# Router logits in four column strips, and steps of the routing moved forward, in a one-core mixer and MoE kernel

## The chip, the cores and the metric

The kernel runs on one core of one Trainium2 chip. The metric is the device time of one execution in microseconds (us).

## The reference

One layer for two sequences, 128 context tokens and 512 latent tokens, with 1024 channels in float32. Each token gets an adaLN-modulated norm, a mixer (mLSTM heads beside a Hyena group, joined by one output projection) and then a hierarchical mixture of 16 experts. What matters here stands between the mixer and the experts:

```python
def rms_norm(x, g):
    y = xf * lax.rsqrt(jnp.mean(xf * xf, axis=-1, keepdims=True) + EPS)
    return y * g
...
x = x + g1 * rms_norm(y, p['g_norm'][1])                  # y: the mixer's output
h = rms_norm(x, p['g_norm'][2]) * (1.0 + sc2) + sh2       # what router and experts read
...
p_coarse = softmax(xt @ p['w_rc'] + p['b_rc'])            # 4 groups, top 1
p_grp, g_idx = lax.top_k(p_coarse, 1)
l_fine = (xt @ p['w_rf'] + p['b_rf']).reshape(t, N_GROUPS, EXPERTS_PER_GROUP)
...
top_l, e_idx = lax.top_k(l_sel, TOP_K_FINE)               # top 2 of the group's 4 experts
w_sel = jax.nn.softmax(top_l, axis=-1) * p_grp
```

So the router has 4 + 16 = 20 logits per token, each a sum over 1024 channels.

## The kernel before, in words

The program is written by hand for each engine, with semaphores `S[...]` between them: TensorE (`pe`), ScalarE (`act`), VectorE (`dve`), GpSimd (`pool`, which issues DMAs) and SyncE (`sp`, which issues the weight loads). `mem` is the SBUF arena ("arena" in the profile), `ps` the eight PSUM banks of 512 float32 columns ("banks"). The 640 tokens are five tiles of 128; the output stage takes them in the order `out_tiles = [0, 3, 2, 4, 1]`, and `j` is the place in that order.

The output stage, about 484 to 563 us of the profiled execution, does for each tile j:

- TensorE: `turn_heads(j)` transposes the heads (L1841), `out_hyena(j)` (L1856) and `out_mlstm(j)` (L1866) form y in two banks, `turn_x2` transposes x2 (L1876), and `logits` (L1887) multiplies h2T, as weights of 128x128, with `wrt` of 20 columns, eight products into 20 columns of bank 7. A float32 product is two instructions. TensorE's order in the loop is `turn_heads(j)`, `turn_x2(j - 2)`, `out_hyena(j)`, `logits(j - 2)`, `out_mlstm(j)`: the logits of a tile come two tiles later. Those of the last two tiles follow after the loop, and then `stay_busy(3)`, products whose result is used by nobody.
- ScalarE: `out_norm(j)` squares both halves of y (L808) and takes the root of their sum (L811); `x2_norm(j)` does the same with x2 (L816, L817); `x2_columns(j, c)` copies the transposed x2 into `h2T` (L823).
- VectorE: `residual(j)` adds the two sums (L1280), takes the reciprocal (L1282) and forms x2 (L1285, L1286); `expert_rows(j)` takes the second reciprocal (L1293) and makes the expert input in two passes of 128x1024 (L1296 multiplies by the norm and a row, L1297 adds a row), which GpSimd's queue stores to DRAM. For the last tile VectorE copies the second half of h2T itself (L1312).

The norm of x2 is not in the logits: they are formed from x2 as it is, with `wrt` scaled by the modulation (L1176, at about 380 us), and VectorE multiplies by the norm when it reads them (L1351).

Then the routing: VectorE sets constants (L1334 to L1339), waits for the logits of all tiles, and finds groups, experts and places, with a few products of TensorE in between (L1917 to L1941, the latter with the 0/1 matrix `fold` that adds four parts of 32 lanes). GpSimd gathers the first rows (L533), and TensorE goes through the groups of 32 tokens, sorted by expert: `gate_and_up` (L1961) and `down` (L1972), with a transpose between (L1980). These use column strips: the weights are 32 tokens, four products stand side by side in the array, and each writes its own quarter of the partitions. SyncE loads the weights of 16 experts in order into three sets of buffers: those of expert 1 after `wo_done` (all tiles projected), of expert 2 after `h2_ready`, of expert e + 3 when expert e is done.

Of the kernel before, what the change touches and what calls it, by code (L numbers as in the profile page):

```python
# [9 lines left out]
ALU = mybir.AluOpType  # L10
ACT = mybir.ActivationFunctionType
# [92 lines left out]
def emit(nc, a, stack):  # L104
# [113 lines left out]
    wrt_lat, wrt_ctx = area(rows1_at, KD, 20), area(cpad_at, KD, 20)  # L218
    shift_sums = area(cpad_at + 160, 2, 20)
# [27 lines left out]
    rbias5 = area(W6 + 960, NT, 20)  # L247
    shifted = area(W1b + 3592, 2, KD, 20)
# [24 lines left out]
    def rt(*shape):  # L273
# [33 lines left out]
        h_ready hsq hss hrs yml_ready yt_done yt_read wo_done wo_sq wo_ss wo_rs x2_sq x2_rs h2_ready h2t_done h2t_read  # L307
# [267 lines left out]
    def _(act):  # L575
# [229 lines left out]
        def out_norm(j):  # L805
            for c in range(2):
                act.wait_ge(S["wo_done"], 2 * j + c + 1)
                link(A(squares[:, c * CH:(c + 1) * CH], ps[:, 1 + 2 * (j % 2) + c, :], ACT.Square,  # L808
                       accum_out=st1[:, 20 + 2 * j + c:21 + 2 * j + c]), "wo_sq")
            act.wait_ge(S["wo_ss"], j + 1)  # L810
            link(A(st1[:, 30 + j:31 + j], st1[:, 30 + j:31 + j], ACT.Sqrt, bias=epsc, scale=1.0 / D), "wo_rs")  # L811
# [7 lines left out]
        def x2_columns(j, c):  # L819
            act.wait_ge(S["h2t_done"], 2 * j + c + 1)  # L820
            if j >= 2:
                act.wait_ge(S["lg_done"], j - 1)
            link(A(h2T[:, j % 2, 4 * c:4 * c + 4, :], ps[:, 5 + c, :].rearrange("p (k t) -> p k t", t=P), ACT.Copy),  # L823
                 "h2t_read")

# [5 lines left out]
        for j in range(NT - 1):  # L831
            x2_norm(j)
            if j == 2:
                out_norm(3)
            for c in range(2):
                x2_columns(j, c)
            if j + 3 < NT:
                heads_square(j + 3)
                heads_root(j + 3)
            if j != 2:  # L840
                out_norm(j + 1)
        x2_columns(NT - 1, 0)
        x2_norm(NT - 1)

# [54 lines left out]
    def _(dve):  # L899
# [275 lines left out]
        for g, scaled in enumerate((wrt_ctx, wrt_lat)):  # L1175
            link(TT(scaled, wrt, pack[:, 1, g, :].unsqueeze(2).broadcast_to((P, KD, 20)), ALU.mult))  # L1176
            link(TT(shifted[:, g], wrt, pack[:, 2, g, :].unsqueeze(2).broadcast_to((P, KD, 20)), ALU.mult))
            link(dve.tensor_reduce(shift_sums[:, g, :], shifted[:, g].rearrange("p k n -> p n k"), AX_X, ALU.add),
                 "consts_ready" if g else "dve_chain")
# [90 lines left out]
        def residual(j):  # L1270
# [7 lines left out]
            dve.wait_ge(S["wo_sq"], 2 * j + 2)  # L1278
            s = st1[:, 30 + j:31 + j]
            link(TT(s, st1[:, 20 + 2 * j:21 + 2 * j], st1[:, 21 + 2 * j:22 + 2 * j], ALU.add), "wo_ss")  # L1280
# [6 lines left out]

        def expert_rows(j):
            t = out_tiles[j]
            rows = row_ctx if t == 0 else row_lat  # L1290
            s = st1[:, 35 + t:36 + t]
            dve.wait_ge(S["x2_rs"], j + 1)
            link(dve.reciprocal(s, s))  # L1293
            if j >= 2:
                dve.wait_ge(h2_stored[j % 2], 16 * (j // 2))
            link(STT(tbuf, x2[:, t, :], s, rows[1], ALU.mult, ALU.mult))  # L1296
            link(TT(h2buf[j % 2], tbuf, rows[2], ALU.add), "h2_ready")  # L1297
# [26 lines left out]
        def over(x, *dims):  # L1324
            return x.broadcast_to((P,) + dims)

# [6 lines left out]
        for coef in (g_coef, e_coef, t_coef):  # L1333
            link(dve.memset(coef, 1.0))  # L1334
            link(dve.memset(coef[:, :, 0:1], 0.0))
        link(dve.tensor_reduce(fold[:, 0:LANE], ident.rearrange("p (q r) -> p r q", q=LANES), AX_X, ALU.add))
        link(CP(fold[:, LANE:].rearrange("p (q r) -> p q r", r=LANE), over(fold[:, 0:LANE].unsqueeze(1), LANES - 1, LANE)))
        link(dve.memset(used, 15.5 / P))
        link(dve.memset(cum, 1.0))  # L1339

# [8 lines left out]
        dve.wait_ge(S["lg_done"], NT)  # L1349
# [135 lines left out]
    def _(pe):  # L1485
# [394 lines left out]
        def logits(j):  # L1880
            t = out_tiles[j]
            w = wrt_lat if t else wrt_ctx
# [14 lines left out]
        for j in range(2, NT):  # L1897
# [3 lines left out]
            logits(j - 2)  # L1901
# [3 lines left out]
        logits(NT - 2)  # L1905
        turn_x2(NT - 1)
        logits(NT - 1)


        def stay_busy(n):  # L1910

            for _ in range(n):
                M(ps[:, 0, :], ident, x2[:, 0, 0:CH], start=True, stop=True)

# [112 lines left out]
```

## Time and profile before

| | us |
|---|---|
| median of three executions | 893.09 (892.60 to 893.87) |
| the profiled execution | 892.52 |
| its span, first to last instruction | 890.7 |
| TensorE busy | 812.8 (91%) |
| VectorE busy | 416.4 (47%) |
| ScalarE busy | 273.8 (31%) |
| GpSimd busy | 105.2 (12%) |

The profile's page sums up one execution. Its views of the trace are the chain of work that ended last (each step followed back to what released it), the timeline of an engine (instructions in order of time, those of one line merged, with the idle time before and what ended it), busy times by stretch with the clock granted to TensorE (1.00 is 2.4 GHz, 0.50 is 1.2 GHz), and the DMA issues with the time to their landing. "x16" is a count of instructions. The time between the span and the execution's own is 1.8 us.

### The profile page before, as it was taken

How to read it: one execution, taken by the hardware profiler on the slowest of the kernel's cores; microseconds unless marked ns; L12 is line 12 of the kernel's file. 1: busy time of each engine (PE TensorE's matmuls, PEld its weight loads, DVE VectorE, ACT ScalarE, POOL GpSimd, SP SyncE). 2: the span in 40 equal slices, each digit the busy share in tenths (PEclk: the TensorE clock that was granted, in tenths of full speed). 3: DMA queues.
4: the chain of work that ended last, by engine and by line, in shares of the span. 5: the costliest groups of instructions: out<-in, count | busy, mean ns of one | idle time of the engine just before them, and what ended most of it. 6: DMA issues, size and time to landing. Idle time of an engine off the chain costs nothing.

```text
span 890.7 us, 17116 instructions
## 1 busy us (share of the span) xinstructions
PE 812.8 (91%) x6809; PEld 442.7 (50%) x6809; DVE 416.4 (47%) x761; ACT 273.8 (31%) x549; POOL 105.2 (12%) x205
## 2 busy tenths in 40 slices
PE   5998999999999999998998999789999999999930
PEld 1242455554554457455764555455555555555510
DVE  5546531123881681753554674733333333333328
ACT  1666321123110311246222233113333333333315
POOL 4000000000001000001001000122222222222131
PEclk9999999999999999998999999699999999999975
DMA  7967450213054503043009204989999999996145
GB/s 256 413 258 273 161 216 0 95 44 146 1 189 149 138 0 107 14 137 100 1 22 368 83 24 183 411 343 416 417 422 419 414 420 419 414 423 281 49 132 239
DMA packets 40201, 191.40 MB, mean 215 GB/s; under 512 B 4416, under 2 KB 4712, under 8 KB 32529
## 3 DMA queue, kind: packets, MB, share of 16 engines
q1 hardware_dynamic: 29146, 155.12, 43.7%
q0 software_dynamic: 8448, 28.99, 9.5%
q10 hardware_dynamic: 2552, 6.50, 2.1%
q8 instruction: 42, 0.69, 0.3%
q14 instruction: 13, 0.11, 0.0%
HBM read 174.14 MB, written 16.44 MB: 214 GB/s over the span
## 4 chain that ended last, share of the span: by engine, by line
PE 82%; DVE 7%; ACT 4%; issue 3%; DMA 2%; POOL 0%; SPq 0%; POOLq 0%; DVEq 0%; ACTq 0%
PE banks L1961 19%; PE banks L1622 16%; PE banks L1972 9%; PE banks L1623 4%; PE banks L1866 4%; PE banks L1856 4%; PE banks L1584 3%; PE banks L1762 3%; PE banks L1771 3%; PE banks L1516 2%; PE banks L1563 2%; ACT arena L763 2%; PE banks L1654 2%; PE banks L1727 2%; PE banks L1980 1%
## 5 line engine op out<-in xcount | busy, mean ns | idle before, releaser
L1961 PE MATMUL banks<-arena 128*32 128x256 f32 x3072 | 175.7, 381 | 1.6 <-DVE arena L1438 1.6
L1622 PE MATMUL banks<-arena 128*128 128x512 f32 x320 | 164.2, 595 | 1.5 <-issue 0.8
L1961 PEld LDWEIGHTS banks<-arena 128*32 128x32 f32 x3072 | 96.2, 110 | 64.7 <-issue 2.6
L1623 PEld LDWEIGHTS banks<-arena 128*128 128x128 f32 x320 | 60.8, 190 | 76.4 <-issue 76.4
L1438 DVE STREAM_TRANSPOSE arena<-arena 128x256 f32<-128x256 f32 x49 | 32.1, 656 | 137.9 <-PE banks L1961 131.5
L1972 PE MATMUL banks<-arena 128*32 128x256 f32 x1536 | 91.7, 379 | 1.0 <-DVE arena L1462 1.0
L1972 PEld LDWEIGHTS banks<-arena 128*32 128x32 f32 x1536 | 50.3, 110 | 33.5 <-DVE arena L1462 1.2
L1623 PE MATMUL banks<-arena 128*128 128x128 f32 x320 | 61.5, 274 | 0.0
L1445 DVE COPY arena<-banks 32x256 f32<-32x256 f32 x98 | 41.4, 422 | 40.8 <-PE banks L1972 40.1
L857 ACT ACTIVATE arena<-banks 32x256 f32<-32x256 f32 x98 | 36.6, 374 | 71.5 <-PE banks L1972 70.9
L1622 PEld LDWEIGHTS banks<-arena 128*128 128x128 f32 x320 | 48.6, 192 | 4.8 <-issue 3.3
L543 POOL DMA_INDIRECT arena<-expert_input,arena x47 | 46.2, 984 | 12.5 <-issue 12.5
L1016 DVE SCALAR_TENSOR_TENSOR arena<-banks,arena 128x504 f32<-128x504 f32 x12 | 8.9, 743 | 73.7 <-ACT arena L690 73.6
L876 ACT ACTIVATE arena<-banks 128x128 f32<-128x128 f32 x48 | 13.3, 277 | 97.7 <-PE banks L1961 97.7
L1771 PE MATMUL banks<-arena 128*128 128x512 f32 x80 | 39.2, 636 | 3.3 <-ACT arena L755 3.3
L873 ACT ACT_TABLE_LOAD x24 | 30.8, 1283 | 30.0 <-DVE arena L1445 23.8
L689 ACT ACTIVATE arena<-banks,arena 128x512 f32<-128x512 f32 x12 | 8.2, 687 | 97.9 <-PE banks L1623 97.9
L1856 PE MATMUL banks<-arena 128*128 128x512 f32 x80 | 35.1, 593 | 2.5 <-ACT arena L755 2.5
L1866 PE MATMUL banks<-arena 128*128 128x512 f32 x80 | 35.5, 597 | 1.7 <-DVE arena L1267 1.7
L1762 PE MATMUL banks<-arena 128*128 128x512 f32 x80 | 36.6, 618 | 0.0
L1584 PE MATMUL banks<-arena 128*128 128x512 f32 x64 | 30.5, 629 | 2.3 <-DVE arena L929 2.3
L540 POOL COPY arena<-arena 128x1 int32 x47 | 8.5, 181 | 182.3 <-DVE arena L1438 182.3
(375 smaller groups left out, 1009.6 us busy)
## 6 DMA issues: line engine op xcount, KB each, us to landing
arena<-in_w_gate SPq DMA_DIRECT2D x16, 2048.0 KB, 21.2
arena<-in_w_up SPq DMA_DIRECT2D x16, 2048.0 KB, 26.9
arena<-in_w_down SPq DMA_DIRECT2D x16, 2048.0 KB, 25.6
arena<-in_w_ada SPq DMA_DIRECT2D x12, 2048.0 KB, 13.2
arena<-in_w_in SPq DMA_DIRECT2D x7, 2048.0 KB, 7.9
expert_output<-arena ACTq DMA_DIRECT2D x49, 128.0 KB, 6.4
expert_output<-arena POOLq DMA_DIRECT2D x1, 4096.0 KB, 20.5
arena<-in_w_out SPq DMA_DIRECT2D x2, 2048.0 KB, 9.0
```

Source lines behind the costliest of these rows:

```text
L543: pool.indirect_dma_start(xr[n], None, h2_quarters, bass.IndirectOffsetOnAxis(ap=idx_now[n], axis=0))\
L857: ins = act.activation(ysb[n][:, l * 256:(l + 1) * 256], ps[l * LANE:(l + 1) * LANE, 5, 0:256], ACT.Copy)
L1445: ins = dve.tensor_copy(ysb[n][:, l * 256:(l + 1) * 256], ps[l * LANE:(l + 1) * LANE, 5, 0:256])
L1584: mm = M(ps[:, b, :], dft_l[:, tb, part, f:f + P], ab[:, part, 1 + tb, :], start=i == 0, stop=i == 1)
L1622: M(ps[:, b, :], lhs, hT[:, k, CTX:TOK], start=k == 0, stop=k == KD - 1)
L1623: mm = M(ps[:, b + 1, 0:CTX], lhs, hT[:, k, 0:CTX], start=k == 0, stop=k == KD - 1)
L1762: mm = M(ps[:, 1 + n % 4, :], hT[:, k, n * P:(n + 1) * P], w[:, k, :], start=k == 0, stop=k == KD - 1)
L1771: mm = M(ps[:, 1, :], hT[:, k, t * P:(t + 1) * P], w[:, k, :], start=k == 0, stop=k == KD - 1)
L1856: M(ps[:, 1 + 2 * (j % 2) + c, :], part1t[:, k, t * P:(t + 1) * P], w[:, NB + k, :], start=k == 0, stop=False)
L1866: mm = M(ps[:, 1 + 2 * (j % 2) + c, :], ymlT[:, k, t * P:(t + 1) * P], w[:, k, :], start=False, stop=k == NB - 1)
L1961: mm = M(ps[q * LANE:(q + 1) * LANE, 2, 0:2 * P].rearrange("p (g f) -> p g f", g=2), xg[:, k, :], gate_up[e % 3][:, :, k, q * P:(q + 1) * ...
L1972: mm = M(ps[l * LANE:(l + 1) * LANE, 5, 0:256], aT[:, q * LANE:(q + 1) * LANE], downs[e % 3][:, q, l * 256:(l + 1) * 256], start=q == 0, s ...
```

## The change

The logits product is turned round: `wrt`, padded from 20 to 32 columns with zeros, is now the weights, and h2T's 128 tokens move. The eight blocks of channels go to four column strips, two blocks to a strip, so each strip holds a part of the logits of all 128 tokens, logits along partitions. ScalarE copies the 128x128 parts to SBUF (`logit_parts`), and one product with `gate_fold`, a 0/1 matrix, adds the four parts and turns the result back to 128 tokens by 20 logits (`logit_sums`). `lg_done` now counts two per tile. Ahead of the last transposes stands a new `stay_busy(2)`.

Beside it: VectorE no longer adds the two sums of squares; it scales the first with 1/D and EPS as soon as it is there, and ScalarE's root takes it as its bias. `expert_rows` is split: x2 times its row (`expert_products`) is formed before the norm is known, and one pass does norm and addition. The routing's constants are set ahead of the last residual instead of behind the last norm. `shift_sums` lies elsewhere, as `wrt` needs more room.

```diff
-    wrt_lat, wrt_ctx = area(rows1_at, KD, 20), area(cpad_at, KD, 20)
+    wrt_lat, wrt_ctx = area(rows1_at, KD, LANE), area(cpad_at, KD, LANE)
...
+    lane_logits = area(W6 + 1100, 2, P)
...
-            link(A(st1[:, 30 + j:31 + j], st1[:, 30 + j:31 + j], ACT.Sqrt, bias=epsc, scale=1.0 / D), "wo_rs")
+            link(A(st1[:, 30 + j:31 + j], st1[:, 21 + 2 * j:22 + 2 * j], ACT.Sqrt, bias=st1[:, 72 + j:73 + j], scale=1.0 / D),
+                 "wo_rs")
...
             if j >= 2:
-                act.wait_ge(S["lg_done"], j - 1)
+                act.wait_ge(S["lg_done"], 2 * (j - 2) + 1)
...
+        def logit_parts(j):
+            act.wait_ge(S["lg_done"], 2 * j + 1)
+            link(A(lane_logits[:, j % 2, :], ps[:, 7, (1 + j % 2) * P:(2 + j % 2) * P], ACT.Copy), "lp_read")
...
             if j != 2:
                 out_norm(j + 1)
+            logit_parts(j)
         x2_columns(NT - 1, 0)
         x2_norm(NT - 1)
+        logit_parts(NT - 1)
...
-            link(TT(scaled, wrt, pack[:, 1, g, :].unsqueeze(2).broadcast_to((P, KD, 20)), ALU.mult))
+            link(dve.memset(scaled[:, :, 20:LANE], 0.0))
+            link(TT(scaled[:, :, 0:20], wrt, pack[:, 1, g, :].unsqueeze(2).broadcast_to((P, KD, 20)), ALU.mult))
...
-            dve.wait_ge(S["wo_sq"], 2 * j + 2)
+            dve.wait_ge(S["wo_sq"], 2 * j + 1)
             s = st1[:, 30 + j:31 + j]
-            link(TT(s, st1[:, 20 + 2 * j:21 + 2 * j], st1[:, 21 + 2 * j:22 + 2 * j], ALU.add), "wo_ss")
+            link(TS(st1[:, 72 + j:73 + j], st1[:, 20 + 2 * j:21 + 2 * j], 1.0 / D, EPS, ALU.mult, ALU.add), "wo_ss")
...
+        def expert_products(j):
+            t = out_tiles[j]
+            link(TT(tbuf, x2[:, t, :], (row_lat if t else row_ctx)[1], ALU.mult))
...
-            link(STT(tbuf, x2[:, t, :], s, rows[1], ALU.mult, ALU.mult))
-            link(TT(h2buf[j % 2], tbuf, rows[2], ALU.add), "h2_ready")
+            link(STT(h2buf[j % 2], tbuf, s, rows[2], ALU.mult, ALU.add), "h2_ready")
...
+            if j == NT - 1:
+                routing_constants()
             residual(j)
+            expert_products(j)
             if j == NT - 1:
                 dve.wait_ge(S["h2t_done"], 2 * NT)
-                dve.wait_ge(S["lg_done"], NT - 2)
+                dve.wait_ge(S["lg_done"], 2 * (NT - 3) + 1)
...
-        dve.wait_ge(S["lg_done"], NT)
+        dve.wait_ge(S["lg_done"], 2 * NT)
...
-        def logits(j):
-            t = out_tiles[j]
-            w = wrt_lat if t else wrt_ctx
+        def logit_strips(j):
+            w = wrt_lat if out_tiles[j] else wrt_ctx
             if j == NT - 1:
                 pe.wait_ge(S["x2_sq"], 2 * NT + 1)
             pe.wait_ge(S["h2t_read"], 2 * j + (1 if j == NT - 1 else 2))
-            for k in range(KD):
-                mm = M(ps[:, 7, 20 * t:20 * t + 20], h2T[:, j % 2, k, :], w[:, k, :], start=k == 0, stop=k == KD - 1)
+            for step in range(KD // LANES):
+                for lane in range(LANES):
+                    k = lane * (KD // LANES) + step
+                    mm = M(ps[lane * LANE:(lane + 1) * LANE, 7, (1 + j % 2) * P:(2 + j % 2) * P], w[:, k, :],
+                           h2T[:, j % 2, k, :], start=step == 0, stop=step == KD // LANES - 1)
             mm.then_inc(S["lg_done"], 1)
+
+        def logit_sums(j):
+            t = out_tiles[j]
+            pe.wait_ge(S["lp_read"], j + 1)
+            M(ps[:, 7, 20 * t:20 * t + 20], lane_logits[:, j % 2, :], gate_fold[:, 0:20], start=True, stop=True)\
+                .then_inc(S["lg_done"], 1)
+
+        def stay_busy(n):
+            for _ in range(n):
+                M(ps[:, 0, :], ident, x2[:, out_tiles[0], 0:CH], start=True, stop=True)
...
             out_hyena(j)
-            logits(j - 2)
+            logit_strips(j - 2)
             if j == NT - 1:
                 turn_x2(j - 1)
             out_mlstm(j)
-        logits(NT - 2)
+            logit_sums(j - 2)
+        logit_strips(NT - 2)
+        stay_busy(2)
+        logit_sums(NT - 2)
         turn_x2(NT - 1)
-        logits(NT - 1)
...
+        logit_strips(NT - 1)
+        logit_sums(NT - 1)
         stay_busy(3)
```

`routing_constants()` holds the ten steps that stood after the last norm, unchanged (six memsets of coefficients, the sum and the copy for `fold`, the memsets of `used` and `cum`).

## Rows read from the trace of the kernel before

**Rows 1.** The page: the chain that ended last by engine, and ScalarE's 128x128 copy.

```profile
PE 82%; DVE 7%; ACT 4%; issue 3%; DMA 2%; POOL 0%; SPq 0%; POOLq 0%; DVEq 0%; ACTq 0%
...
L876 ACT ACTIVATE arena<-banks 128x128 f32<-128x128 f32 x48 | 13.3, 277 | 97.7 <-PE banks L1961 97.7
```

**Rows 2.** The chain in order of time, 500 to 550: start, us, what.

```profile
508.25 1.70 PE banks L1887 x16
...
525.08 1.70 PE banks L1887 x16
...
541.91 1.69 PE banks L1887 x16
```

**Rows 3.** The same chain, tail of the last tile.

```profile
552.53 0.30 ACT arena L811
...
555.42 0.70 DVE arena L1286
```

**Rows 4.** VectorE's timeline: start, us, line, operation, [idle before, by whom ended].

```profile
383.74 2.82 DVE L1186 TENSOR_TENSOR arena<-arena 128x2560 f32<-128x2560 f32 x1 [1.71 <-DMA arena<-running_max]
...
552.28 0.16 DVE L1280 TENSOR_TENSOR arena<-arena 128x1 f32<-128x1 f32 x1 [9.02 <-ACT arena L808]
...
557.38 0.69 DVE L1312 COPY arena<-banks 128x512 f32<-128x512 f32 x1 [1.26 <-PE banks L1876]
...
559.62 1.23 DVE L1297 TENSOR_TENSOR arena<-arena 128x1024 f32<-128x1024 f32 x1
...
562.94 0.26 DVE L1351 TENSOR_TENSOR arena<-banks,arena 128x100 f32<-128x100 f32 x1
```

**Rows 5.** The chain from the first gather into the expert groups.

```profile
576.02 7.26 DMA arena<-expert_input,arena
...
594.56 0.26 PE banks L1980
```

**Rows 6.** TensorE's timeline: tail, routing, then expert groups.

```profile
558.12 3.60 PE L1887 MATMUL banks<-arena 128*128 128x20 f32 x16 [0.84 <-DVE arena L1312]
561.56 5.47 PE L1913 MATMUL banks<-arena 128*128 128x512 f32 x6
567.90 0.45 PE L1917 MATMUL banks<-arena 128*128 128x80 f32 x2 [0.87 <-DVE arena L1368]
...
572.83 0.36 PE L1937 MATMUL banks<-arena 128*32 128x8 f32 x20 [2.11 <-DVE arena L1395]
...
578.62 0.43 PE L1941 MATMUL banks<-arena 128*128 128x64 f32 x2 [0.51 <-DVE arena L1403]
...
589.18 1.07 PE L1961 MATMUL banks<-arena 128*32 128x256 f32 x16
...
622.64 3.66 PE L1961 MATMUL banks<-arena 128*32 128x256 f32 x64
...
628.22 3.66 PE L1961 MATMUL banks<-arena 128*32 128x256 f32 x64
```

**Rows 7.** Busy by stretch: PE, PEld, DVE, ACT, POOL, clock, DMA share, GB/s.

```profile
554.00:556.00 2.00, 1.12 (x4) 0.72 (x4) 1.93 (x3) 0.14 (x1) 0.00 (x0) 0.50 1.08 453
```

**Rows 8.** SyncE's timeline: when the loads are asked for.

```profile
561.24 0.43 SPq L434 DMA_DIRECT2D arena<-in_w_up  x1
...
575.55 0.81 SPq L437 DMA_DIRECT2D arena<-modulation_rows  x2
592.89 0.33 SPq L442 DMA_DIRECT2D arena<-in_w_gate  x1
...
604.43 0.45 SPq L442 DMA_DIRECT2D arena<-in_w_up  x1
```

**Rows 9.** Landing of loads asked for at 561.24, 575.55, 604.43; last column us.

```profile
arena<-in_w_up SPq DMA_DIRECT2D x1, 2048.0 KB, 22.9
...
arena<-modulation_rows SPq DMA_DIRECT2D x2, 512.0 KB, 15.7
...
arena<-in_w_up SPq DMA_DIRECT2D x1, 2048.0 KB, 20.3
```

More of the change, by code:

```diff
@@ L216, in emit @@
     assert at <= WORDS, at
-    wrt_lat, wrt_ctx = area(rows1_at, KD, 20), area(cpad_at, KD, 20)
-    shift_sums = area(cpad_at + 160, 2, 20)
+    wrt_lat, wrt_ctx = area(rows1_at, KD, LANE), area(cpad_at, KD, LANE)
+    shift_sums = gate_taps.rearrange("p a b c d -> p (a b c d)")[:, 0:40].rearrange("p (g n) -> p g n", g=2)
     ada_rows = [area(W1 + 6144, CH), area(W4, CH), area(W4 + CH, CH)]
@@ L306, in emit @@
         e_ready w_ready s_done p_ready kw_ready inter_done inter_read intra_done num_ready upd_done st_ready
-        h_ready hsq hss hrs yml_ready yt_done yt_read wo_done wo_sq wo_ss wo_rs x2_sq x2_rs h2_ready h2t_done h2t_read
+        h_ready hsq hss hrs yml_ready yt_done yt_read wo_done wo_sq wo_ss wo_rs x2_sq x2_rs h2_ready h2t_done h2t_read lp_read
         lg_done rt_v rt_exp pos_done idx_done tiles_ready route_ready
@@ L1286, in residual @@
                 link(TT(x2[:, t, half], x2[:, t, half], tbuf[:, half], ALU.add), "x2_sq")
+        def expert_products(j):
+            t = out_tiles[j]
+            link(TT(tbuf, x2[:, t, :], (row_lat if t else row_ctx)[1], ALU.mult))
         def expert_rows(j):
             t = out_tiles[j]
-            rows = row_ctx if t == 0 else row_lat
+            rows = row_lat if t else row_ctx
             s = st1[:, 35 + t:36 + t]
@@ L1295, in expert_rows, with over, routing_constants @@
                 dve.wait_ge(h2_stored[j % 2], 16 * (j // 2))
-            link(STT(tbuf, x2[:, t, :], s, rows[1], ALU.mult, ALU.mult))
-            link(TT(h2buf[j % 2], tbuf, rows[2], ALU.add), "h2_ready")
+            link(STT(h2buf[j % 2], tbuf, s, rows[2], ALU.mult, ALU.add), "h2_ready")
+        def over(x, *dims):
+            return x.broadcast_to((P,) + dims)
+        def routing_constants():
+            for coef in (g_coef, e_coef, t_coef):
+                link(dve.memset(coef, 1.0))
+                link(dve.memset(coef[:, :, 0:1], 0.0))
+            link(dve.tensor_reduce(fold[:, 0:LANE], ident.rearrange("p (q r) -> p r q", q=LANES), AX_X, ALU.add))
+            link(CP(fold[:, LANE:].rearrange("p (q r) -> p q r", r=LANE), over(fold[:, 0:LANE].unsqueeze(1), LANES - 1, LANE)))
+            link(dve.memset(used, 15.5 / P))
+            link(dve.memset(cum, 1.0))
         heads_norm(0)
@@ L1322, in _ @@
         dve.wait_ge(h2_stored[1], 16 * 2)
-        def over(x, *dims):
-            return x.broadcast_to((P,) + dims)
         r4, r16, groups = rconst[:, 0:4], rconst[:, 4:20], rconst[:, 20:20 + GROUPS + 2]
@@ L1332, in _ @@
         pk, sl, grp = rt(2, NT), rt(2, NT), rt(2, NT)
[L1333 to L1339, printed above, removed]
         def flat(x):
@@ L1904, in _ @@
             out_mlstm(j)
-        logits(NT - 2)
+            logit_sums(j - 2)
+        logit_strips(NT - 2)
+        stay_busy(2)
+        logit_sums(NT - 2)
         turn_x2(NT - 1)
-        logits(NT - 1)
-        def stay_busy(n):
-            for _ in range(n):
-                M(ps[:, 0, :], ident, x2[:, 0, 0:CH], start=True, stop=True)
+        logit_strips(NT - 1)
+        logit_sums(NT - 1)
         stay_busy(3)
```

## The prediction

> **What bounds the kernel now.** I read the page first: TensorE (PE) carries 82% of the chain that ended last [rows 1]. Then the chain itself, in order of time, for the stretch that the diff touches. From 493 to 551 us it is TensorE alone, one token tile after another at 525.08 - 508.25 = 16.8 us each, and the logits of tiles 0 to 2 stand in it with 1.70, 1.70 and 1.69 us [rows 2]. So what leaves TensorE here moves everything behind it. From 551.4 on the chain changes its nature: the last tile runs through ScalarE (ACT), VectorE (DVE) and TensorE by turns [rows 3, 4]; at 562.94 VectorE starts on the routing, alone but for short products, up to the first gather at 576.02, which lands after 7.26 us [rows 5]. Then TensorE works through the expert groups, 628.22 - 622.64 = 5.58 us each, without a wait [rows 6]. So I look for two sums: what leaves TensorE before 551.4 (A), and by how much the routing starts earlier after that (B). Everything later should only move, if the weight stream lets it.
>
> **A, the loop over tiles.** Removed are the logits of tiles 0, 1 and 2: 1.70 + 1.70 + 1.69 = 5.09 us. Those of tile 3 lie beside the wait for the last residual, and tile 4's belong to B. Their 16 instructions (two for each of eight products) start 0.11 us apart, with 128 weight columns and only 20 moving: it is the weight loads that are paid.
> Added are three times 16 strip matmuls, 128x32 weights and 128 moving columns. The nearest row is the expert product L1961, the same strips with 256 moving columns: 64 take 3.66 us and 16 take 1.07, so (3.66 - 1.07) / 48 = 54 ns each. Half the columns give 27 ns if columns set the pace, 54 if something else does. That nothing else holds it at 54 is seen in L1937: 20 strip matmuls with 8 columns in 0.36 us, at most 18 ns each [rows 6]. So a strip product costs 16 x 27 = 0.43, and I add 0.17 for the change of shape around it: one full-array transpose between two strip products (L1980) holds the chain for 0.26 [rows 5], of which about 0.11 is its own load. Together 0.60 (ends 0.43 and 1.03, the latter at 54 ns).
> Added too is the folding product, 2 instructions with 128x128 weights: 2 x 0.11 = 0.22. Those of tiles 0 and 1 stand ahead of 551.4; tile 2's stands behind the last mLSTM product, where TensorE waits. A = 5.09 - 3 x 0.60 - 2 x 0.22 = 2.85 us (ends 1.6 and 3.4).
>
> The Trainium skill, page "TensorEngine Tiling (Array Packing)", section Tiling Modes, says that a change of tiling mode drains TensorE, which speaks against a strip product set between full-array ones. The trace agrees but puts little on it: L1980 between two strip products costs some 0.15 us over its own load.
> The skill's page "TensorE: Matmul & The Clock Gate", section "Wait — 56ns, not 53.3ns?", says that with hardware decoding off each matmul costs the sequencer about 62 ns. By it a strip product would be 16 x 62 = 1.0 us and A about 1.65; the 18 ns of L1937 say that this does not bind here.
>
> The new waits in the loop. ScalarE gets `logit_parts` (128x128 out of PSUM, 0.28 by L876 [rows 1]), which waits for the strips. For tiles 0 and 1 it stands behind `out_norm`, and the next thing in its queue, `x2_norm`, has to wait longer anyway. For tile 2 it stands ahead of `x2_norm(3)`, which ran before the logits of tile 2 and must now wait until the strips are done. Behind it queue the copies of tile 3 and VectorE's second norm; TensorE needs those copies only for the logits of tile 3 at 551.2, some 8 us later, so I cost it at nothing (2 us, the length of the delay, if that cover were gone). `logit_sums(j)` waits for a copy made 7 us before. VectorE's `expert_products` replaces one of two passes one for one. The two extra memsets of `wrt`, about 0.1 us each, fall in front of an idle 1.71 us at 383.74 that a DMA ends [rows 4]: nothing. No step is moved on the queues of SP or GpSimd, but their triggers (`wo_done`, `h2_ready`) come earlier.
>
> **B, the tail,** on the old clock, with the end of the last mLSTM product at 551.4 fixed.
> - The sum of the two squares leaves the path: the square root may start when the second square is read out, about 552.20, instead of 552.53 [rows 3]. So -0.33, and the last half of x2 is done at 555.79 instead of 556.12.
> - `stay_busy(2)` after the strips of tile 3: fold 0.22, strips 0.60, 4 x 0.43 (512 columns), fold 0.22, to 554.2. The first transposes wait for x2 until about 554.3. It just fits, and as the second transposes (555.8) are the ones that count, 1 us more costs nothing.
> - The product of x2 with its row (128x1024, 1.23 by L1297 [rows 4]) runs from 555.8 to 557.05 beside the transposes; the copy L1312 starts at 557.08 instead of 557.38 and ends at 557.8. Then reciprocal and one pass instead of two: VectorE is free at 559.3 instead of 560.86.
> - Ten memsets and copies of constants fill 560.9 to 562.9 [rows 4]. They go to the idle 9.02 us ahead of L1280, the last residual: -2.0. What is late next is the logits.
> - Logits: strips from 557.85. At full clock 0.43 and about 0.3 to come out, copy 0.28, fold 0.43 (L1941 [rows 6]): with hand-overs 559.4. But the clock granted was 0.50 from 554 on [rows 7], after TensorE had had little to do since 551.4, and the 16 logits instructions took 3.60 instead of 1.70 us [rows 2, 6]. At that level 560.0, and at 54 ns doubled 560.9. `stay_busy(2)` puts the fall off by 2 to 3 us, so the transposes should be fast, and the strips may go either way.
> So the routing starts between 559.3 (VectorE's own bound) and 560.9. I take 559.75, between the results of the two clock levels: B = 562.94 - 559.75 = 3.2 (ends 2.0 and 3.65). Against it: `stay_busy(3)`, 5.47 us at the low clock [rows 6], now starts together with the routing, whose first question to TensorE comes 567.90 - 562.94 = 4.96 us later; it used to begin 1.4 us ahead of it. I take 0.15 off (ends 0 and 0.5).
> Sum: 2.85 + 3.2 - 0.15 = 5.9 us.
>
> **Does the rest move along?** The weights of experts 1 and 2 are asked for from 551.4 and 560.9, and the DMA engines are full from then on [rows 7, 8]. That backlog ends with the modulation rows, 575.55 + 15.7 = 591.3 us, and the next load is asked for at 592.89: 1.6 to spare [rows 8, 9]. The change starts the backlog 2.85 earlier but asks for the next load 5.9 earlier: the stream falls 3.05 - 1.6 = 1.45 us behind. The tightest later need is expert 4's up weights: asked for at 604.43, landed 20.3 later at 624.7, used at 628.22, so 3.5 to spare [rows 6, 8, 9]. 1.45 fits in; nothing is given back.
>
> **The rivals.**
> - *The gather eats the tail.* If the first gather lands by what lies ahead of it in the full DMA engines, it comes only A earlier: 893.1 - 2.85 = 890.2. For it: 7.26 us for a small transfer. Against: it landed at 583.3, ahead of the up weights asked for 15 us before it (561.24 + 22.9 = 584.1 [rows 8, 9]), so it does not queue behind them. Chance 0.13.
> - *The pace of the old loads stays.* If a strip matmul still costs 0.11 us, a strip product is 1.76, A = 5.09 - 5.28 - 0.44 = -0.6 and B, at the low clock, about 0.8: 892.9, no change. Against: the 18 ns of L1937. 0.08.
> - *Slower: the strips run one after another.* If in `logit_strips` four strips with 128 moving columns do not overlap, each costs some 0.22 us, half of L1941's two in 0.43 [rows 6]: 3.5 a tile, three times in the loop and once in the tail. A = 5.09 - 10.5 - 0.44 = -5.9, B = 3.2 - 2.5 = 0.7: with the 0.15, 898.4. It decides from 0.12 us per instruction (64 of them on the path have 5.9 us to lose). L1961 at 54 ns with double the columns speaks against it. 0.05.
> - *Both sums at their low ends* (A 1.6, B 2.0, 0.5 lost): 890.0. 0.12.
>
> **How the numbers follow.** The profiled execution took 892.52 us (span 890.7), 0.57 under the median of 893.09, which is within what executions differ; I take the 5.9 us off the median: 887.2. The forecast, a gain of 4 to 7, has 0.62, and the four cases above 0.38. Range 885.8 to 890.9: from both high ends together (7.05, and 0.2 for the measurement) to just past the two cases at 890. About 0.2% (1.8 us) is what a measurement of this kernel can tell from no change: faster 0.87, same 0.08, slower 0.05.
>
> **What would show it.** Strip products of some 0.6 us in the TensorE timeline and tiles of 15.9 instead of 16.8 us; the square root right behind the square; VectorE waiting 0 to 1 us for TensorE between the last norm and the routing; the gather still 7.3 us from issue to landing; groups of 5.58 us with no wait. Wrong would be: strip products of 1.7 us or more, a gather of 9 us or longer, a stall at expert 4 (the stream over 3.5 us behind), or a low clock that begins before the last transposes.

## The result, and the profile after

| | before | changed |
|---|---|---|
| median, 4 executions each (us) | 892.85 (890.74 to 893.87) | 885.57 (884.86 to 886.38) |
| ratio | | 0.992 (0.9902 to 0.9939) |
| profiled execution, its span (us) | 892.52, 890.7 | 886.38, 884.5 |

By the ratio the change is 7.1 us faster, with 5.4 to 8.7 as the interval; forecast were 5.9. The time of 885.57 lies 0.23 us below the range. In the two profiled executions the change gives 5.1 us behind the point where it begins to act, so the sum was a little too large and not too small; the other 2 us look like scatter between executions, which the runs make likely but do not prove. One execution of one kernel below (no_warm) took 1102.72 us at a mean granted clock of 0.743 and is left out of every comparison.

The chain of the changed kernel where the tiles run (start, us, what); L1905 is a strip product, L1912 a folding product, L1883 the mLSTM product, to be held against [rows 2]:

```profile
507.63 0.57 PE banks L1905 x16
508.21 7.06 PE banks L1883 x16
515.27 0.13 PE banks L1912 x2
...
523.62 0.57 PE banks L1905 x16
...
539.61 0.57 PE banks L1905 x16
540.19 1.02 PE banks L1893 x8
541.21 6.88 PE banks L1883 x16
```

1.70 us of logits have become 0.57, and a tile takes 523.62 - 507.63 = 16.0 us instead of 16.8. VectorE's timeline in the tail, against [rows 4]:

```profile
549.29 0.16 DVE L1291 RECIPROCAL arena<-arena 128x1 f32<-128x1 f32 x1 [2.99 <-ACT arena L812]
...
553.77 0.69 DVE L1340 COPY arena<-banks 128x512 f32<-128x512 f32 x1
...
554.70 1.28 DVE L1309 SCALAR_TENSOR_TENSOR arena<-arena 128x1024 f32<-128x1024 f32 x1
556.22 0.26 DVE L1368 TENSOR_TENSOR arena<-banks,arena 128x100 f32<-128x100 f32 x1 [0.24 <-PE banks L1912]
...
576.53 0.64 DVE L1455 STREAM_TRANSPOSE arena<-arena 128x256 f32<-128x256 f32 x1 [2.73 <-DMA arena<-expert_input,arena]
```

The ten constants are gone from between the last pass and the routing (L1368), and 0.24 us of waiting for the folding product are left. TensorE's timeline from the last transposes to the first expert group, against [rows 6]:

```profile
552.54 0.66 PE L1893 MATMUL banks<-arena 128*128 128x128 f32 x4 [0.86 <-DVE arena L1295]
554.52 0.65 PE L1905 MATMUL banks<-arena 128*32 128x128 f32 x16 [1.32 <-DVE arena L1340]
555.62 0.40 PE L1912 MATMUL banks<-arena 128*128 128x20 f32 x2 [0.46 <-ACT arena L830]
...
567.53 3.76 PE L1917 MATMUL banks<-arena 128*128 128x512 f32 x4
571.23 0.86 PE L1963 MATMUL banks<-arena 128*32 128x64 f32 x20
572.51 0.69 PE L1967 MATMUL banks<-arena 128*128 128x64 f32 x2 [0.42 <-DVE arena L1420]
572.99 5.61 PE L1917 MATMUL banks<-arena 128*128 128x512 f32 x8
578.53 3.66 PE L1987 MATMUL banks<-arena 128*32 128x256 f32 x64
```

Here is something that was not so before. The eight instructions of `stay_busy(4)` (L1917) run into the first group: VectorE has turned the gathered rows by 577.2, but the group starts at 578.53. By stretch, in the columns of [rows 7] (the clock is the third from the end), the changed kernel shows why:

```profile
564.00:566.00 2.00, 0.01 (x1) 0.00 (x0) 1.76 (x8) 0.00 (x0) 0.00 (x0) 1.00 1.02 420
566.00:568.00 2.00, 1.28 (x23) 1.19 (x24) 1.65 (x11) 0.00 (x0) 0.00 (x0) 0.67 1.03 424
...
574.00:576.00 2.00, 2.00 (x4) 0.96 (x3) 0.00 (x0) 0.00 (x0) 0.00 (x0) 0.50 1.06 430
```

TensorE has nothing to do from 564 to 566, then the clock falls to the lower level (0.50 is 1.2 GHz), and products that are there only to keep it up take longer and stand in the way. The clock fell at this place in the kernel before too, but there it was back early enough. Its TensorE timeline, and one stretch with the clock:

```profile
574.05 3.55 PE L1913 MATMUL banks<-arena 128*128 128x512 f32 x4
...
578.90 3.65 PE L1913 MATMUL banks<-arena 128*128 128x512 f32 x8
```

```profile
574.00:576.00 2.00, 2.00 (x5) 0.98 (x5) 1.72 (x9) 0.00 (x0) 0.00 (x0) 0.57 0.95 410
```

By stretches of half a microsecond the clock was low from 574.1 to 577.6 before (3.5 us) and from 566.7 to 576.6 in the changed kernel (9.9 us). So it is the length of the low stretch that differs, and with it the last eight instructions: 3.65 us before, 5.61 now.

To compare kernels piece by piece I measure from S, the start of the first tile's mLSTM product (484.51 before, 483.89 after); the kernel before has this one trace, so every comparison with it rests on one execution. Three recorded expectations call this point "the second tile's" product; it is the same point. All in us after S, from the timelines:

| | last mLSTM product done | routing starts | gather issued | VectorE turns it | first group | last `down` |
|---|---|---|---|---|---|---|
| before | 66.88 | 78.43 | 91.51 | 98.79 | 99.68 | 368.03 |
| changed | 64.19 | 72.33 | 85.41 | 92.64 | 94.64 | 362.94 |
| gain | 2.69 | 6.10 | 6.10 | 6.15 | 5.04 | 5.09 |

So all that the change does is worth 5.1 us in these two executions. The rest of the 6.2 by which the spans differ lies ahead of S (0.62) and in the last stage (0.5).

### The profile page after: what moved, and what is told of

The parts are those of the page before. It is cut to its first block, busy times and chain, and to the rows that moved or that the text cites. A ratio compares the mean times of both kernels' runs of the same rounds, so it can differ in the third digit from the quotient of the medians.

```text
span 884.5 us, 17156 instructions
## 1 busy us (share of the span) xinstructions
PE 808.7 (91%) x6823; PEld 435.0 (49%) x6823; DVE 416.9 (47%) x763; ACT 275.8 (31%) x554; POOL 105.5 (12%) x205
## 4 chain that ended last, share of the span: by engine, by line
PE 83%; DVE 6%; ACT 4%; issue 3%; DMA 2%; POOL 0%; ACTq 0%; POOLq 0%; DVEq 0%
PE banks L1987 19%; PE banks L1639 16%; PE banks L1998 9%; PE banks L1640 4%; PE banks L1883 4%; PE banks L1873 4%; PE banks L1601 3%; PE banks L1779 3%; PE banks L1788 3%; PE banks L1533 2%; PE banks L1580 2%; ACT arena L764 2%; PE banks L1671 2%; PE banks L1744 2%; PE banks L2006 1%
## 5 line engine op out<-in xcount | busy, mean ns | idle before, releaser
L1883 PE MATMUL banks<-arena 128*128 128x512 f32 x80 | 35.6, 597 | 1.7 <-DVE arena L1276 1.7
```

The costliest lines, as they stand in the source:

```text
L1883: mm = M(ps[:, 1 + 2 * (j % 2) + c, :], ymlT[:, k, t * P:(t + 1) * P], w[:, k, :], start=False, stop=k == NB - 1)
```

## Experiments

Every kernel is the changed one with the edit shown. Each ratio is to executions of the kernel before on the same chip: their medians were 891.53 us for the first four rows, 892.68 for the next three and 891.76 for the last four. (The ratios differ a little from those of the medians: for after_again the medians give 0.9952.) Times of whole executions scatter by several us (below), so each expectation is judged by the points after S, in one trace of each kernel.

| kernel | median | ratio to before | last mLSTM | routing | first group | last `down` |
|---|---|---|---|---|---|---|
| after_again | 887.23 | 0.9941 (0.9918 to 0.9963) | 64.18 | 72.33 | 94.62 | 362.92 |
| old_logits | 888.53 | 0.9954 (0.9934 to 0.9975) | 66.88 | 75.49 | 97.91 | 366.21 |
| late_constants | 886.78 | 0.9941 (0.9920 to 0.9962) | 64.18 | 74.18 | 95.55 | 363.86 |
| short_busy | 885.86 | 0.9927 (0.9907 to 0.9947) | 64.18 | 72.33 | 94.08 | 362.37 |
| early_registers | 888.19 | 0.9951 (0.9933 to 0.9968) | 64.19 | 72.33 | 95.23 | 364.02 |
| old_norms | 886.89 | 0.9941 (0.9920 to 0.9962) | 64.19 | 73.37 | 94.81 | 363.10 |
| late_loads | 888.65 | 0.9953 (0.9937 to 0.9970) | 64.18 | 72.33 | 95.15 | 364.37 |
| fill_gap | 885.89 | 0.9924 (0.9896 to 0.9952) | 64.18 | 72.33 | 93.48 | 361.77 |
| combined | 886.97 | 0.9956 (0.9935 to 0.9976) | 64.19 | 72.33 | 93.72 | 364.33 |
| no_warm_again | 885.68 (one) | | 64.19 | 72.98 | 94.20 | 362.49 |
| double_strips | 883.09 (one) | | 65.50 | 74.30 | 95.60 | 363.97 |

**The same kernel again.**

> The changed kernel unchanged, for the size of its gain and to be beside the other kernels on one chip. Theory one (the sum of steps 5.9 us was right and the other 1.4 is scatter of the executions): 5.5 to 6.5 us below the kernel before. Theory two (a term was under-sized): 7 us or more below it. In the trace: last mLSTM product to routing 8.1 us, gather 7.2 us from issue to use.

By the ratio it came out 5.3 us below the kernel before (3.3 to 7.3): just under theory one's 5.5. Theory two's 7 lies at the edge of the interval, so whole executions alone do not exclude it. After S its trace repeats the first one to 0.02 us at every point; but S itself is at 486.81 instead of 483.89. The two intervals, 5.4 to 8.7 and 3.3 to 7.3, overlap around the 5.1 of the trace and the forecast 5.9. Where does S move? Four instructions of a product early in the kernel, in after_again and in late_constants, which are the same program there:

```profile
44.69 3.78 PE L1601 MATMUL banks<-arena 128*128 128x512 f32 x4 [1.12 <-DVE arena L937]
```

```profile
44.70 1.98 PE L1600 MATMUL banks<-arena 128*128 128x512 f32 x4 [1.13 <-DVE arena L937]
```

And eight products behind an idle 3.3 us further on, by TensorE's timeline, first in the changed kernel, then in double_strips; the program is the same up to there:

```profile
414.05 6.58 PE L1788 MATMUL banks<-arena 128*128 128x512 f32 x8 [3.37 <-ACT arena L756]
```

```profile
412.45 3.67 PE L1788 MATMUL banks<-arena 128*128 128x512 f32 x8 [3.33 <-ACT arena L756]
```

The same four products take 3.78 or 1.98 us behind the same idle 1.1 us, and the same eight 6.58 or 3.67 us. S lay between 479.4 and 486.8 us in the traces of this study. That is a scatter of 7 us ahead of anything that the change touches, from how long the clock stays low behind a few short idle stretches. Why it falls in one execution and not in another was not tested. Whole executions scatter as widely: 18 of the kernel before on one chip took 888.31 to 896.97 us. All 50 of the kernel before on record have a median of 892.1, the ten of the changed kernel (four above, six here) 886.7: 5.4 us apart, near the 5.1 of the traces.

**Strips undone.**

```diff
-            logit_strips(j - 2)
+            logits(j - 2)
...
-            logit_sums(j - 2)
```

(and `logit_parts` removed, the products of the last two tiles likewise)

> The changed kernel with the logits product of before, all else as changed (norms, constants, the extra stay_busy(2)). Theory one (strips pay in the loop 2.7 us and in the tail about what the low clock makes of 16 weight loads): tiles of 16.8 us again, the routing starts 0.3 us later in the tail at full clock, 2.3 at the low clock: 3.0 to 5.0 us slower than the changed kernel. Rival (the tail is bound by VectorE's own passes): 2.7 us slower and no more.

The last mLSTM product is back at 66.88, 2.69 later, exactly where the kernel before has it, so A comes from the strips, their fold and their copy, and nothing else. In the tail 0.47 more is lost (8.61 us from that product to the routing instead of 8.14), and the last group ends 3.27 later, inside theory one's 3.0 to 5.0. The clock was high there: the 16 old logits instructions took 1.96 us, as TensorE's timeline of old_logits shows, against 0.65 for strips plus a copy and a fold.

```profile
557.65 1.96 PE L1898 MATMUL banks<-arena 128*128 128x20 f32 x16 [1.33 <-DVE arena L1334]
```

**Strips doubled.**

```diff
-            for step in range(KD // LANES):
+            for step in list(range(KD // LANES)) * (2 if j < NT - 2 else 1):
```

> The changed kernel with each strip product of tiles 0 to 2 done twice, for the price of 16 strip matmuls without the change of shape around them. Theory one (columns set the pace, 27 ns each, and the change of shape costs the rest): each strip product takes 0.43 us more, 1.00 instead of 0.57, and the last mLSTM product ends 1.3 us later after the second tile's. Rival (the change of shape costs nothing, an instruction costs 36 ns): 0.57 more, 1.7 in all.

TensorE's timeline: 32 instructions in 1.08 us, where 16 took 0.65.

```profile
503.04 1.08 PE L1905 MATMUL banks<-arena 128*32 128x128 f32 x32
```

(65.50 - 64.18) / 48 = 27.5 ns per strip matmul: theory one. Columns set the pace (27.5 ns for 128, 54 for 256 in [rows 6]), four strips side by side, and 0.57 - 0.44 = 0.13 us of a strip product is what is left for the change of shape. Its total of 883.09 is below every execution of the changed kernel although it does more work. That is the scatter again: S was at 479.37.

Two more things stand in this trace. The strips of the last tile, which are not doubled and stand behind `stay_busy(2)`, took 1.08 us and their fold 0.62, since the clock had fallen at 551, and the routing started 8.80 us after the last mLSTM product instead of 8.14:

```profile
551.31 1.08 PE L1905 MATMUL banks<-arena 128*32 128x128 f32 x16 [1.33 <-DVE arena L1340]
```

And in the routing the clock was low for 3.3 us only, and the first group followed VectorE's transpose by 0.30 us: nothing was held by `stay_busy(4)` in this execution.

**Constants back.**

```diff
-            if j == NT - 1:
-                routing_constants()
...
         dve.wait_ge(h2_stored[1], 16 * 2)
+        routing_constants()
```

> The changed kernel with the routing's constants back behind the last norm. Theory one: VectorE is at 555.98 when it would begin them, so the routing starts at 558.0 instead of 556.2, 1.8 us later, and the whole is 1.8 us slower. Rival (the first expert group is held by stay_busy(4) and not by the gather, as in the profiled execution, by 1.1 us): only about 0.8 us slower.

The routing starts 1.85 later, as expected, but the first group only 0.91 later and the last `down` 0.92: the rival. VectorE's timeline of late_constants, the first constant and the routing:

```profile
554.70 0.07 DVE L1317 MEMSET arena<- 128x20 f32 x1
...
556.72 0.26 DVE L1367 TENSOR_TENSOR arena<-banks,arena 128x100 f32<-128x100 f32 x1
```

Half of what moving the constants gives is given back before the first group, in these two executions.

**Norms back.**

```diff
-            expert_products(j)
...
-            link(STT(h2buf[j % 2], tbuf, s, rows[2], ALU.mult, ALU.add), "h2_ready")
+            link(STT(tbuf, x2[:, t, :], s, rows[1], ALU.mult, ALU.mult))
+            link(TT(h2buf[j % 2], tbuf, rows[2], ALU.add), "h2_ready")
```

(and the sum of squares ahead of the root)

> The changed kernel with the norms of before (sum of the two squares by VectorE ahead of the root, and norm times row and plus row in two passes after the root). Theory one: the root starts 0.3 us later, the copy of the transposes 0.2 us earlier (no product stands ahead of it), and VectorE with two passes is ready 0.8 us later than the changed kernel, so the routing starts about 8.95 us after the last mLSTM product instead of 8.15. Rival (the logits chain is what is last, and VectorE has time to spare): 0.3 us or less.

The routing starts 9.18 after the last mLSTM product instead of 8.14, so 1.04 later; theory one, with 0.23 more than expected. The copy L1340 did come 0.16 earlier after S; but VectorE then waited 0.17 for ScalarE's root, and the second pass costs its whole 1.23. The first group starts only 0.17 later. Again the gain is not kept. The three parts taken back one at a time move the start of the routing by 0.47 (old logits), 1.85 (constants) and 1.04 us (norms), 3.36 together, where the change as a whole moved it by 3.41 against the last mLSTM product.

**The last stay_busy cut.**

```diff
-        stay_busy(4)
+        stay_busy(2)
```

> The changed kernel with the last stay_busy(4) cut to 2. In the profiled execution the four products ran at the low clock, 5.6 us, and ended 1.1 us after the gather was turned. Theory one: that held the first group, so 0.5 to 1.1 us faster, with the first group starting 0.3 us after VectorE's transpose. Rival: the clock is low when the first group comes, which then takes up to 3.6 us more: 1 to 3 us slower.

The first group starts 0.56 earlier (theory one's 0.5 to 1.1), and the clock was back at 1.00 by then, so the rival is out. But the group does not follow the transpose by 0.25 us as in the kernel before. VectorE's transpose ended at 577.14; TensorE's timeline:

```profile
578.07 3.66 PE L1987 MATMUL banks<-arena 128*32 128x256 f32 x64 [1.21 <-DVE arena L1455]
```

**Register loads moved ahead.**

```diff
+        pe.wait_ge(S["tiles_ready"], 2)
+        first += first_groups(8, NE + 1)
         row_numbers(later, EARLY, 6)
-        stay_busy(4)
-        pe.wait_ge(S["tiles_ready"], 2)
-        first += first_groups(8, NE + 1)
+        stay_busy(2)
```

> The changed kernel with TensorE's last nine register loads moved ahead of the second row-number products, and the last stay_busy(4) cut to 2. In every run so far the first expert group starts 5.4 to 6.0 us after the last folding product, whatever the gather does, and with stay_busy(2) TensorE stood idle for 0.9 us after VectorE's transpose. Theory one: the register loads behind the product are that time; then the group follows the transpose by 0.25 us as in the kernel before, and starts 0.7 us earlier than with stay_busy cut alone, 1.1 to 1.2 earlier than in the changed kernel. Rival: the code of the expert loop is what is waited for, and the 0.9 us stay.

A miss: the group starts 0.6 later than in the changed kernel. TensorE's timeline says where the loads went:

```profile
572.33 0.86 PE L1963 MATMUL banks<-arena 128*32 128x64 f32 x20 [2.40 <-issue]
```

The nine register loads hold TensorE's queue for 2.4 us ahead of the row numbers, which come that much later, and `stay_busy(2)` behind them again stands in front of the group. The loads are a real cost, but this place is worse. In the three kernels with the loads moved (this one and the last two below) the row numbers start 89.7 to 89.8 us after S, which is 4.8 to 4.9 us after VectorE's last cast, the value that the loads wait for; the products ahead of them end at 87.4 in two of the three and at 85.4 in the third. So nine loads take about 4.8 us from when their value is there, partly beside products that are still running.

**stay_busy(2) in the tail removed.**

```diff
         logit_strips(NT - 2)
-        stay_busy(2)
```

> The changed kernel without the stay_busy(2) ahead of the last tile's transposes. Theory one: TensorE's clock falls before the last strips, as it fell before the last logits of the kernel before; transposes take 1.1 instead of 0.7 us, the strips 1.2 instead of 0.65, and the routing starts 0.6 to 1.0 us later than 8.15 us after the last mLSTM product. Rival: the clock holds without it and nothing moves.

> The changed kernel without the stay_busy(2) ahead of the last tile's transposes, one look at its trace. Theory one: the clock falls before the last strips, the routing starts 0.6 to 1.0 us later than 8.15 us after the last mLSTM product. Rival: the clock holds without it.

The first gave five executions with a median of 885.83 us, a ratio of 0.9936 (0.9915 to 0.9957); the second gave one execution, with the trace. TensorE's timeline, the last strips and their fold:

```profile
554.31 1.08 PE L1905 MATMUL banks<-arena 128*32 128x128 f32 x16 [1.26 <-DVE arena L1340]
555.85 0.61 PE L1912 MATMUL banks<-arena 128*128 128x20 f32 x2 [0.46 <-ACT arena L830]
```

Strips and fold take 1.08 and 0.61 instead of 0.65 and 0.40, and the routing starts 8.79 after the last mLSTM product, 0.65 later: theory one's number, at its lower end. But double_strips, which keeps this `stay_busy(2)`, has the same 1.08, 0.62 and 8.80. With the two products in place the clock held through the last tile's logits in ten traces of eleven, all but double_strips; without them it fell in the only trace. That they hold the clock is therefore likely and not shown. And the first group starts 0.44 earlier than in the changed kernel, since in this execution the clock did not fall at the row numbers but stayed at 1.00 to the group.

**The gap in the routing filled.**

```diff
-        stay_busy(2)
+        stay_busy(4)
         pe.wait_ge(S["tiles_ready"], 1)
```

> The changed kernel with stay_busy(4) instead of 2 ahead of the first row numbers, where TensorE stood idle for 2.1 us (564.0 to 566.2 in the changed kernel) just before its clock fell. Theory one (that idle time is what drops the clock, and the low clock from 566 on holds the first group): the clock stays at 1.00 up to the group, the last stay_busy(4) takes 3.6 instead of 5.6 us, and the first group starts 0.9 to 1.2 us earlier, 93.5 us after the second tile's mLSTM product instead of 94.64. Rival (the clock falls anyway, or the four products end too late for the row numbers): the group no earlier, or 0.5 us later.

Theory one, at its upper end. TensorE's timeline of fill_gap, and under it one stretch with the clock (third from the end):

```profile
560.26 3.68 PE L1917 MATMUL banks<-arena 128*128 128x512 f32 x8
564.36 0.36 PE L1963 MATMUL banks<-arena 128*32 128x8 f32 x20 [0.42 <-DVE arena L1412]
...
570.03 3.65 PE L1917 MATMUL banks<-arena 128*128 128x512 f32 x8
575.60 3.66 PE L1987 MATMUL banks<-arena 128*32 128x256 f32 x64 [1.92 <-DVE arena L1455]
```

```profile
566.00:568.00 2.00, 1.52 (x4) 0.38 (x2) 1.76 (x8) 0.00 (x0) 0.47 (x1) 1.00 1.08 455
```

The idle time ahead of the row numbers shrinks from 2.15 to 0.42 us, the clock did not fall there and stays at 1.00 from 558 on, the last `stay_busy(4)` takes 3.65 instead of 5.61, and the group starts when VectorE has turned the gathered rows: 1.16 earlier after S, and the last `down` 1.17 earlier. One trace could be luck, but the others agree: with 2.1 to 2.2 us idle at this place the clock fell within 1.4 us after it in eight of nine traces, and with 0.4 to 0.7 us idle (fill_gap, combined, late_constants, old_norms) in none of four; in the last two it had been low just before, so they say less. By the points after S this is the best kernel of the study, 6.26 us better than the kernel before; by whole executions (885.89, ratio 0.9924) it can't be told from the changed one.

**The gather alone.** early_registers, and

```diff
+        sp.wait_ge(h2_stored[0], 16 * 3)
+        sp.wait_ge(S["tiles_ready"], 2)
+        sp.wait_ge(gather[0], 16)
         for i, (dst, src, full) in enumerate(expert(2)):
-            if i == 2:
-                sp.wait_ge(h2_stored[0], 16 * 3)
             sp.dma_start(dst, src).then_inc(full, 16)
-        sp.wait_ge(S["tiles_ready"], 2)
```

> early_registers, with the weights of expert 2 asked for only when the first gather has landed, so that the DMA engines have little else to do during the gather. Theory one (the gather's 7.2 us are mostly sharing with the weight stream): it takes 3 to 4.5 us from issue to VectorE's transpose and the first group starts about 3 us earlier; but the stream then lies some 7 to 9 us behind its demand, more than the 3.5 us to spare at expert 4, and TensorE waits 3 to 5 us there: no gain in all. Rival (the 7.2 us are the gather's own latency): it stays above 6.5 us.

SyncE asks for the weights as soon as the gather has landed, so its timeline, under GpSimd's, gives the time:

```profile
569.16 1.28 POOL L534 DMA_INDIRECT arena<-expert_input,arena  x1 [12.49 <-issue]
```

```profile
572.37 0.33 SPq L436 DMA_DIRECT2D arena<-in_w_gate  x1
```

3.2 us from issue to landing instead of 7.2: the gather's time is mostly the weight stream's, as theory one had it (the DMA share was 0.32 and 0.23 from 568 to 572, 1.07 and 1.09 in the changed kernel). The rest of theory one missed. The first group starts 0.5 later than in the changed kernel, not 3 earlier, as TensorE's row numbers, behind the register loads, came later and VectorE waited for them; and TensorE waited only 0.29 us at expert 4, not 3 to 5.

**All together.** fill_gap, early_registers, late_loads, and the last `stay_busy(1)`.

> fill_gap, early register loads, the last stay_busy cut to 1, and the weights of expert 2 asked for when the first gather has landed. In late_loads the gather had landed 3.2 us after its issue instead of 7.2, but TensorE was held by its own stay_busy(2) at the low clock. Theory one: with TensorE free, VectorE's transpose follows its last row numbers and the first group starts 2 to 3.5 us earlier than in the changed kernel (91 to 92.6 us after the second tile's mLSTM product); expert 4 then waits 1 to 3 us for its weights, so the last group ends 0.5 to 2 us earlier. Rival: something else in TensorE's queue (its loads of registers and code) keeps the start at 94 us.

Nearer the rival's 94 than theory one's 91 to 92.6. The first group starts at 93.72, between fill_gap and the changed kernel, and the last `down` 1.4 us after the changed kernel's. TensorE's timeline:

```profile
572.15 0.85 PE L1963 MATMUL banks<-arena 128*32 128x64 f32 x20 [4.34 <-issue]
...
576.15 4.98 PE L1987 MATMUL banks<-arena 128*32 128x256 f32 x64 [0.22 <-DVE arena L1455]
...
622.51 3.66 PE L1987 MATMUL banks<-arena 128*32 128x256 f32 x64 [0.93 <-DMA arena<-in_w_up]
```

The register loads hold the queue for 4.34 us in which TensorE does nothing; the clock falls in that time (0.52 from 572 to 574, 0.50 after it), and the first group takes 4.98 instead of 3.66. In fill_gap, with the loads in their old place, the same row numbers start 3.0 us earlier after S. Expert 4 waits 0.93 us for its weights.

## Why the prediction missed, point by point

- **A**: forecast 2.85, measured 2.69 (66.88 - 64.19), and old_logits gives all of it back. The strip product was put at 0.60 and takes 0.57; the pace of 27 ns holds (27.5 in double_strips). The fold was put at 0.22 and takes 0.13 to 0.17. The new waits in the loop cost nothing, as forecast: TensorE has no idle time between the tiles' products from 500 to 548. What the sum left out is that the full-array work behind is slower by a little: 7.06 instead of 6.96 for an mLSTM product, 1.02 instead of 0.92 for the transposes behind the third strips.
- **B**: forecast 3.2, measured 3.41 (11.55 - 8.14). The square root starts 548.90 - 548.18 = 0.72 after the last square instead of 1.04: 0.32, forecast 0.33. The constants, as forecast, went to idle time. The clock stayed high for the last strips, so the better of the two cases came true; where it fell, the routing starts 0.65 later (no_warm_again, and double_strips with `stay_busy(2)` in place), so this part of B is in part luck. The forecast compared 3.60 us of old logits at the low clock with 1.70 at the high one, from two different views; the timeline that shows 3.60 has 1.86.
- **stay_busy(3)**: 0.15 taken off, measured nothing: the routing takes 13.08 us up to the gather in both kernels.
- **Together** up to the routing: 6.10 gained, where 2.85 + 3.2 - 0.15 = 5.9 was forecast. Part of the agreement is luck, as A fell 0.16 short and B came out 0.21 above.
- **What the prediction lacked**: the last `stay_busy(4)`, which its sum does not mention. In the kernel before the gather was what came last, and the products ahead of it were covered. In the changed kernel the low clock in the routing lasted 9.9 us instead of 3.5, the eight instructions took 5.61 instead of 3.65 us, and of the 6.10 only 5.04 reached the first group. (VectorE's transpose came 6.15 earlier, as the gather was 0.05 shorter; the transpose to the group is 1.11 longer.) fill_gap gets this back with no other edit. In the text, this is the step "everything later should only move, if the weight stream lets it": the stream did let it, and TensorE's own filling did not. With this term the sum is 2.69 + 3.41 - 1.06 = 5.04, where 5.9 was forecast. The term depends on the execution: it is there in both traces of the changed kernel, and missing in double_strips and no_warm_again, where the clock was low for 3.3 us or not at all. Why the low stretch is longer in one execution than in another stays open.
- **The stream**: forecast 1.45 us behind its demand, with 3.5 to spare at expert 4. The modulation rows landed 20.0 us after their issue at 568.84, at 588.8; the next load was asked for at 587.24, so 1.6 behind, and no group waited. The DMA issues of the changed kernel:

```profile
arena<-modulation_rows SPq DMA_DIRECT2D x2, 512.0 KB, 20.0
```

- **The gather**: 7.23 us from issue to use, 7.28 before. The rival "the gather eats the tail" is out, though its premise was half right: the full DMA engines do cost the gather 4 us (late_loads), but 7.28 us from issue to use before and 7.23 after say that this was so in both kernels.
- **The pace of the old loads, and the strips one after another**: both out, by 27.5 ns. The Trainium skill, page "TensorE: Matmul & The Clock Gate", section "Wait — 56ns, not 53.3ns?", gives about 62 ns per matmul for the sequencer with hardware decoding off; this kernel's strips start at less than half of that, so that floor does not bind here; no run shows which decoding was on. The Trainium skill, page "TensorEngine Tiling (Array Packing)", section Tiling Modes, says that a change of mode drains the engine: the trace agrees that the change costs something, 0.13 us a strip product plus the 0.10 by which the product behind it is longer, but no run shows the drain itself apart.
- **The range**: this is the step that put the measured time outside. Its low end was both high ends of A and B and, in the prediction's words, "0.2 for the measurement", when the three executions of the kernel before lay within 1.3 us. But S alone lay anywhere within 7 us from trace to trace, by the clock in stages far ahead of the change, and the median of four drawn from the 50 executions of the kernel before lies up to 1.6 us from their own in 19 of 20 draws. The base had drawn high: 893.09, where the 50 have 892.1. The four executions of the changed kernel had drawn low: 885.57, where the ten have 886.7, which lies inside the range. Read so, the measured 7.1 (5.4 to 8.7) and 5.3 (3.3 to 7.3) are both the 5.1 of the traces; that the two whole-execution results differ by scatter alone is argued from these numbers, since only one execution of each series has a trace. By the same reckoning, an estimate, the low end belonged near 884.

## What to carry to other kernels

Where a product has a full 128x128 operand as weights and only some 20 columns moving, try it the other way round, with the narrow operand as the weights in column strips: here 16 instructions went from 1.70 to 0.57 us, and copy and fold could wait for a place where TensorE doesn't. Products put in to keep TensorE's clock up are work on a deadline: after every gain ahead of them, look again at whether the clock holds up to them and at what stands behind them, since at the lower clock they take up to twice as long (four took 3.76 us instead of 1.96) and hold what follows. And before giving a range from whole executions, look at where the profile starts to differ: measure from a point just ahead of the change, and give the scatter in front of it as a term of its own.

## What was not expected of the hardware

- Nine register loads in TensorE's queue take about 4.8 us from when their value is there, in three kernels. Where products run beside them they show as 2.4 us of idle time, and where little does as 4.34. They fit the 0.93 us by which the first group trailed the transpose in short_busy, where it was 0.25 before. That the loads and not the fetching of code are that time was argued from where the gap moved with them, not shown apart.
- The small gather takes 3.2 us when the DMA engines have little else to do and 7.2 beside the weight stream.
- With 2.1 to 2.2 us of idle time at the same place ahead of the row numbers the clock fell in eight traces and not in no_warm_again, and it then stayed low for 3.3 us (double_strips) to 13.6 us (late_loads). What decides either stays open. That filling the idle time held the clock there is shown by fill_gap and combined, with two kernels whose idle time was short for other reasons.
